# Recurrence of an RWKV-7 layer on one core: chain in two sets of eight heads, state update in two accumulating parts

## What is computed

```python
def step(S, inp):
    r_t, d_t, k_t, v_t, a_t, b_t = inp
    sa = jnp.einsum('bhij,bhj->bhi', S, a_t)
    S = (S * d_t[:, :, None, :] + sa[..., None] * b_t[:, :, None, :]
         + v_t[..., None] * k_t[:, :, None, :])
    return S, jnp.einsum('bhij,bhj->bhi', S, r_t)
```

## Time and profile before

| | us |
|---|---|
| median of 3 runs | 1520.93 (1519.63 to 1522.9) |
| profiled execution, its own time | 1519.45 |
| span of its trace | 1517.7 |
| TensorE busy | 1413.9 (93%) |
| VectorE busy | 928.3 (61%) |
| ScalarE busy | 754.1 (50%) |
| mean granted TensorE clock | 0.958 |
| recurrence, first sb to last y | 140.62 to 273.51 |

### The profile page before, as it was taken

One profiled execution on the slowest core, in us unless ns is written; L12 is line 12 of the kernel. 1 busy time (PEld: TensorE's weight loads), 2 busy tenths in 40 slices (PEclk: granted clock), 3 DMA queues, 4 the chain that ended last, 5 costly groups with the idle time before them and its releaser, 6 DMA issues.

```text
span 1517.7 us, 27277 instructions
## 1 busy us (share of the span) xinstructions
PE 1413.9 (93%) x11109; PEld 1266.0 (83%) x11109; DVE 928.3 (61%) x1355; ACT 754.1 (50%) x1166; POOL 43.9 (3%) x79
## 2 busy tenths in 40 slices
PE   5988988789999898899998999999999998899998
PEld 4867988379999787799997898799997787789997
DVE  6847332666676757666767465755557566565554
ACT  4562321165555755655557464544445464454443
POOL 5000000010000000000000000010001000000000
PEclk9998988599999999999999999999999999999999
DMA  7420001455555440555554554556654543245550
GB/s 221 135 103 1 4 3 44 166 155 193 188 172 194 142 168 25 186 203 193 167 193 147 186 185 148 164 174 191 193 187 146 178 165 102 84 159 180 190 191 29
DMA packets 135073, 222.25 MB, mean 146 GB/s; under 512 B 6137, under 2 KB 105697, under 8 KB 134720
## 3 DMA queue, kind: packets, MB, share of 16 engines
q1 hardware_dynamic: 132688, 214.19, 43.4%
q0 software_dynamic: 2144, 6.61, 1.4%
q10 hardware_dynamic: 144, 0.06, 0.0%
HBM read 219.77 MB, written 1.05 MB: 145 GB/s over the span
## 4 chain that ended last, share of the span: by engine, by line
PE 84%; DVE 9%; ACT 5%; issue 2%; DMA 1%; SPq 0%; DVEq 0%; ACTq 0%
PE ps L477 81%; DVE ulo L463 1%; ACT uhi L455 1%; DVE scratch L1799 1%; PE ps L771 1%; DVE x_sb L1773 1%; DMA raw<-in_w_rkv 1%; PE ps L1082 0%; DVE scratch L2087 0%; DVE xn_lo L1761 0%; DVE xs L1749 0%; ACT scratch L1310 0%; DVE x_sb L1779 0%; PE ps L918 0%; ACT xn_hi L1341 0%
## 5 line engine op out<-in xcount | busy, mean ns | idle before, releaser
L463 DVE TENSOR_TENSOR ulo<-raw,uhi 128x1024 fp32r<-128x1024 f32 x400 | 488.3, 1224 | 383.4 <-ACT uhi L455 383.1
L455 ACT ACTIVATE uhi<-raw 128x1024 fp32r<-128x1024 f32 x400 | 422.7, 1059 | 442.8 <-PE ps L477 437.5
L477 PE MATMUL ps<-xn_hi,uhi 128*128 128x256 f32 x1472 | 418.0, 284 | 6.7 <-DVE xn_lo L1815 2.6
L477 PE MATMUL ps<-xn_lo,uhi 128*128 128x256 f32 x1472 | 416.5, 283 | 0.0
L477 PE MATMUL ps<-xn_hi,ulo 128*128 128x256 f32 x1472 | 416.4, 283 | 0.0
L477 PEld LDWEIGHTS ps<-xn_hi,uhi 128*128 128x128 f32 x1472 | 282.3, 192 | 10.5 <-issue 4.0
L477 PEld LDWEIGHTS ps<-xn_lo,uhi 128*128 128x128 f32 x1472 | 282.4, 192 | 1.7
L477 PEld LDWEIGHTS ps<-xn_hi,ulo 128*128 128x128 f32 x1472 | 282.3, 192 | 0.0
L477 PE MATMUL ps<-uhi,xm_hi 128*128 128x512 f32 x512 | 201.3, 393 | 1.8 <-DVE xm_lo L2035 1.1
L477 PE MATMUL ps<-ulo,xm_hi 128*128 128x512 f32 x512 | 200.6, 392 | 0.0
L477 PE MATMUL ps<-uhi,xm_lo 128*128 128x512 f32 x512 | 159.9, 391 | 0.0
(11 more groups left out here) (273 smaller groups left out, 1331.2 us busy)
## 6 DMA issues: line engine op xcount, KB each, us to landing
raw<-in_mlp_w SPq DMA_DIRECT2D x64, 1024.0 KB, 5.3
raw<-in_w_up SPq DMA_DIRECT2D x44, 1024.0 KB, 5.1
raw<-in_w_down SPq DMA_DIRECT2D x22, 1024.0 KB, 4.9
raw<-in_gmlp_w_in SPq DMA_DIRECT2D x16, 1024.0 KB, 5.4
raw<-in_fox_w_in SPq DMA_DIRECT2D x16, 1024.0 KB, 5.3
raw<-in_w_rkv SPq DMA_DIRECT2D x12, 1024.0 KB, 6.2
raw<-in_gmlp_w_out SPq DMA_DIRECT2D x8, 1024.0 KB, 4.8
raw<-in_w_o_rwkv SPq DMA_DIRECT2D x4, 1024.0 KB, 5.9
```

What stands on the lines that cost most here:

```text
L455: nc.scalar.activation(ring_unit(uhi, m, n), raw_unit(n, j), ACT.Copy).then_inc(hi_done, 1)
L463: nc.vector.tensor_tensor(ring_unit(ulo, m, n), raw_unit(n, j), ring_unit(uhi, m, n).bitcast(F32), ALU.subtract).then_inc(lo_done, 1)
L477: return nc.tensor.matmul(o, l, r, start=start, stop=stop, skip_group_check=True)
```

## The change

- `rs`, `ys`, `y` and `st` are cut into two sets of eight heads (g = 0, 1) as `u` was. VectorE's part of `rs` and `st` is cut likewise (four head pairs per instruction instead of eight), so each set's chain needs only its own set's results.
- `st` becomes two stages: `sv` (keys x values, needs no solution) opens the accumulation in a ring bank, and `st` (rates x solution) closes it in the same bank; only `st` is moved out.
- The list is written anew: u0 goes in after two stages of `prepare(1)` instead of five, then a part after every five; for chunks 2 and 3 a fixed order is written out, in which `sv`, `ys` and `y` of one set stand between dependent steps of the other, and y2.1 stands after u3.

The list grows from 94 stages to 113. No arithmetic is added: the matmuls are the same in number and size.

```diff
--- before.py
+++ after.py
@@ -137,19 +137,31 @@
                 [x for g in both for x in st("l2", [g]) + st("z1", [g])] + st("z2"))
 
     def advance(c):
-        first = [("rs", c, 0), ("ys", c, 0)] if c else []
-        return [first, [("u", c, 0), ("u", c, 1)], [("y", c, 0)] + ([("st", c, 0)] if c < 3 else [])]
-
-    stages = [("kn", q, 0) for q in range(4)] + [("bonus", 0, 0)] + prepare(0)
+        def both(name):
+            return [(name, c, 0), (name, c, 1)]
+
+        state = [st for g in (0, 1) for st in (("sv", c, g), ("st", c, g))]
+        return [both("rs") + both("ys") if c else [], both("u"), state + both("y")]
+
+    first = prepare(0)
+    stages = [("kn", q, 0) for q in range(4)] + [("bonus", 0, 0)] + first
     ahead = [part for c in (0, 1) for part in advance(c) if part]
     rest = prepare(1)
+    take = 2
     while rest:
-        stages += rest[:5]
-        rest = rest[5:]
+        stages += rest[:take]
+        rest = rest[take:]
+        take = 5
         if ahead:
             stages += ahead.pop(0)
-    for part in ahead + advance(2) + advance(3):
+    for part in ahead:
         stages += part
+
+    def eight(name, c):
+        return [(name, c, 0), (name, c, 1)]
+
+    stages += eight("rs", 2) + eight("sv", 2) + eight("u", 2) + eight("ys", 2) + eight("st", 2) + [("y", 2, 0)]
+    stages += eight("rs", 3) + eight("ys", 3) + eight("u", 3) + [("y", 2, 1)] + eight("y", 3)
     return stages
 
 
@@ -279,6 +291,10 @@
         ring_bank, ring_use, ring_total = {}, {}, [0] * 4
         turn = 0
         for k, st in enumerate(stages):
+            if st[0] == "st":
+                n = stage_no[("sv", st[1], st[2])]
+                ring_bank[k], ring_use[k] = ring_bank[n], ring_use[n]
+                continue
             ring_bank[k], ring_use[k] = [], []
             for _ in range(CORE_BANKS.get(st[0], 1)):
                 b = turn % 4
@@ -920,31 +936,33 @@
                 else:
                     n, hh, c = i // 2, halves[i % 2], slice(64 * i, 64 * i + 64)
                     if name in ("rs", "ys"):
-                        wait_moved(("st", i - 1, 0))
+                        wait_moved(("st", i - 1, g))
                         if name == "rs":
-                            for q in range(2):
-                                wait_moved(("rv", n, q))
+                            wait_moved(("rv", n, g))
                         else:
                             pe.wait_ge(core_ps, stage_no[("yk", n, 1)] + 1)
-                        for j in range(8):
+                        for j in range(4 * g, 4 * g + 4):
                             for u in range(2):
                                 oo = o[u] if name == "rs" else bank(2 * n + u)
                                 last = mm(oo[hh, HD * j:HD * j + HD], (at_ if name == "rs" else rt)[halves[u], j, c],
                                           S0[halves[u], j, :], name == "rs", name == "rs")
                     elif name == "u":
                         wait_moved(("z2", n, g))
-                        wait_moved(("rs", i, 0) if i else ("rv", n, g))
+                        wait_moved(("rs", i, g) if i else ("rv", n, g))
                         for e in range(8):
                             head = 8 * g + e
                             last = mm(o[0][hh, HD * e:HD * e + HD], core_kept(n, g, "TT")[hh, e // 2, e % 2, :],
                                       by_head(core_u(n))[hh, head, :], True, True)
                     else:
-                        for q in range(2):
-                            wait_moved(("u", i, q))
-                            wait_moved(("tok" if name == "st" else "sb", n, q))
+                        if name != "sv":
+                            wait_moved(("u", i, g))
+                        else:
+                            for q in range(2):
+                                wait_moved(("tok", n, q))
                         if name == "y":
-                            pe.wait_ge(core_ps, stage_no[("ys", i, 0) if i else ("yk", n, 1)] + 1)
-                        for j in range(8):
+                            wait_moved(("sb", n, g))
+                            pe.wait_ge(core_ps, stage_no[("ys", i, 1) if i else ("yk", n, 1)] + 1)
+                        for j in range(4 * g, 4 * g + 4):
                             for u in range(2):
                                 head = 2 * j + u
                                 hc = slice(HD * head, HD * head + HD)
@@ -954,8 +972,10 @@
                                     last = mm(oo, core_kept(n, j // 4, "ArbT")[hh, j % 4, u, :], U, False, True)
                                 else:
                                     oo = o[0][halves[u], HD * j:HD * j + HD]
-                                    mm(oo, core_tok(n, 1)[hh, hc], V, True, False)
-                                    last = mm(oo, core_tok(n, 0)[hh, hc], U, False, True)
+                                    if name == "sv":
+                                        last = mm(oo, core_tok(n, 1)[hh, hc], V, j == 4 * g, False)
+                                    else:
+                                        last = mm(oo, core_tok(n, 0)[hh, hc], U, False, True)
                 last.then_inc(core_ps, 1)
 
             for st in stages[5:]:
@@ -1923,18 +1943,20 @@
                     continue
                 if name == "rs":
                     hh = slice(64 * (i % 2), 64 * (i % 2) + 64)
+                    js = slice(4 * g, 4 * g + 4)
                     for u in range(2):
-                        r = by_pair(core_u(i // 2))[hh, :, u, :]
-                        TT(r, r, by_head(o[u])[hh], ALU.add).then_inc(moved[ring_bank[k][u]], 1)
+                        r = by_pair(core_u(i // 2))[hh, js, u, :]
+                        TT(r, r, by_head(o[u])[hh, js], ALU.add).then_inc(moved[ring_bank[k][u]], 1)
                     continue
                 o8 = by_head(o[0])
                 if name == "st":
-                    scale = eS[:, :, i:i + 1].to_broadcast([P, 8, HD])
+                    js = slice(4 * g, 4 * g + 4)
+                    scale = eS[:, js, i:i + 1].to_broadcast([P, 4, HD])
                     if i == 0:
-                        ins = TT(S0, o8, scale, ALU.mult)
+                        ins = TT(S0[:, js], o8[:, js], scale, ALU.mult)
                     else:
-                        step(TT(S0, o8, S0, ALU.add))
-                        ins = TT(S0, S0, scale, ALU.mult)
+                        step(TT(S0[:, js], o8[:, js], S0[:, js], ALU.add))
+                        ins = TT(S0[:, js], S0[:, js], scale, ALU.mult)
                 else:
                     dst, a = {"x1": ("X", "X"), "x2": ("X", "X"), "x3": ("Z", "X"), "z1": ("Z1", "Z"),
                               "z2": (None, "Z1")}[name]
```

## The result

| | before | with the change |
|---|---|---|
| median of 6 runs, us | 1520.85 (1519.56 to 1523.7) | 1508.56 (1506.34 to 1511.07) |
| ratio, 95% interval | | 0.9915 (0.990 to 0.993) |
| profiled execution, own time | 1519.45 | 1509.0 |
| its span | 1517.7 | 1507.3 |
| list of stages | 94 | 113 |

By the medians the kernel is 12.3 us faster; 1508.0 was forecast. The two profiled executions differ by 10.4 us of span. All of that lies between VectorE's first piece of sb1.0 and its first of the normalisation (from here on **the stretch**): 188.78 to 273.51 before, 188.85 to 263.05 now. Behind it the same 26.4 us pass, and the rest of the program takes as long as before.

A forecast was written before the change was run, and what follows sets the result against it. It took TensorE's recurrence chain, its pauses and the half-clock stretches after them, as the bound. -5.8 + 1.1 - 9.3 = -14.0 gave 1505.4, as median 1506.9; 1.1 given back made 1508.0, range 1503.0 to 1516.0 (own case 1503.5 to 1512).

The forecast's parts named there:

- What bounds it, and how it reaches the end: Recurrence up to 273.51: TensorE's chain bounds it; time saved there passes whole through the 26.4 us behind.
- Term A: First slow stretch, after 193.54: u0 moved into earlier pauses leaves the path and TensorE's clock stays up, -5.8 us.
- Term B: Middle, st0 to y1: same work in twice the stages, one new pause ahead of rs1.1, +1.1 us, bounds 0 and 2.2.
- the instruction pause: TensorE's 1.92 us stop at 237.63 inside xn1.1, taken for late instructions: kept unchanged, bounds -1.9 and +1.9 us.
- rival 1: TensorE's clock falls as it did, so only u0's move and shorter pauses gain: -5.1 us, 1515.8, chance 0.14.
- Term C: Chunks 2 and 3: 23.8 us become 14.5 at full clock with 1.2 us of pauses left, -9.3 us.
- VectorE's half pieces: VectorE's 64 x 256 pieces of rs taken at 0.4 us each; the upper end would add 1.0 us.
- The 19 added stages at nothing: The added stage ends, each with a semaphore increment and up to four waits, cost nothing; by the skill 0.5 us.
- 2 (the halves don't overlap): Each of 19 added stages stands exposed for 0.94 us: +3.9 us, 1524.8, slower than before, chance 0.05.
- 3: u0 waits for its bank until VectorE drained sb1.1, so the first slow stretch stays: -8.2 us, 1512.7, chance 0.06.
- 4: Nothing reaches the end, because the projection behind the recurrence waits for a load instead: 1521, chance 0.03.
- The signs: Clock 1.00 from 193; chunks 2 and 3 in 14 to 16 us; L1961 near 259.5; 26.4 behind; 1.1 pause before rs1.1.

The follow-up runs named there:

- u0_early: The kernel before with only u0.0 and u0.1 moved to after two stages of the second half's preparation instead of five: median 1515.92 us, ratio 0.9987.
- rows_late: The changed kernel with POOL's three row loads into gb issued after stage u3.0 instead of yk1.1: median 1503.06 us, ratio 0.9883 to the kernel before.
- rows_late_before: The kernel before with only POOL's three row loads into gb moved from yk1.1 to after u3.0: median 1515.27 us, ratio 0.9966.
- u0_late: The changed kernel with u0.0 and u0.1 put back behind five stages of preparation: median 1508.79 us, ratio 0.9926 to the kernel before.
- plain_tail: The changed kernel with chunks 2 and 3 in the old order, still cut into sets: median 1510.36 us, ratio 0.9933 to the kernel before.
- pads: The kernel before with 104 products by a zero matrix (208 records) put in TensorE's pauses: median 1511.79 us, ratio 0.9942.

## Why the prediction was right, and where it was off

- **What bounds it, and how it reaches the end.** Right. 10.5 us went in the stretch of the profiled execution, and the 26.4 us behind it passed on all but 0.1.
- **Term A, -5.8.** By the trace right: from VectorE's drain to the end of a2, 188.78 to 206.3 before and 188.85 to 200.3 now, 6.0 us less. The assumption under it, that the clock stays up over what is left of the pauses, held in four traces with an early u0 and failed for 3.4 us in a fifth (u0_early). In the medians of runs the term is not confirmed: u0_early can't be told from no change, and u0_late isn't slower than the changed kernel.
- **Term B, +1.1.** From a2's end to rs2.0 it is 43.1 us before, 48.6 now: +5.5. Its own part was about right, though the one pause that it is added up from is 0.77 us and not 1.1: with the loads moved away in both kernels, the middle takes 42.2 us (rows_late) against 40.9 (rows_late_before), +1.3. The failing step is the one on **the instruction pause**, "I keep it": it grew by 1.3 us, and the step said nothing of the clock behind it. TensorE was busy 5.8 of 6.8 us at 0.50; at 24 ns of every 54 that is 2.6 us more, 3.9 us together. The bound (+1.9) had only the pause in it, though the first paragraph of the prediction says that a pause costs twice. The prediction's one argument on that clock (under rival 1) was that it had stayed up over the 1.92 us; it did so over 3.01 us in u0_early too, but not over 3.24 here, 3.04 in u0_late, 2.96 in plain_tail and 2.65 in pads. What decides that stays open. That the pause comes from the loads could have been read ahead: the queues' packets are in the same trace.
- **Term C, -9.3.** 24.1 us before, 14.1 now: -10.0. Two pauses of 0.40 and 0.43 remain, 0.8 us where 1.2 were taken. But the prediction gave the gain to the order of the stages as much as to the cutting; the order is worth 0.6 us by the traces.
- **VectorE's half pieces, 0.4 taken.** Right:

```profile
249.75 0.73 DVE L1949 TENSOR_TENSOR scratch<-scratch,ps 64x256 f32<-64x256 f32 x2
```

- **The 19 added stages at nothing.** Right: chunks 2 and 3 take 14.1 us less 0.8 of pauses, which is the 13.3 us of their records alone, and in rows_late TensorE is busy 64.36 of 67.84 us over all of the stages. The Trainium skill ("TensorE: Matmul & The Clock Gate", "The cost: per-tile semaphore tail") names 26.3 ns for each increment. The trace shows none of it; here each increment stands behind 16 records or more.
- **The rivals.** 1 (the clock falls as it did) is out by the trace. 2 (the halves don't overlap) is out: plain_tail has the halves back to back, with nothing open behind u2 and u3, where 0.94 stood before, and 0.40, 0.26 and 0.25 us elsewhere. 3 and 4 are out.
- **The sum.** -14.0 against -10.5 measured in the profiled pair; 3.9 us are the instruction pause and its slow stretch, 0.5 more went in the middle, and A and C gave 0.9 more. So the profiled execution took 1509.0 where the sum gave 1505.4. That the median, 1508.6, lies 0.6 us from the forecast is in part luck: the 1.1 us given back had another reason, and the executions of one kernel differ by 5 us.
- **The range.** Its upper end, 1512, isn't the sum of the terms named for it: 1508.0 + 1.0 + 1.1 + 1.9 + 2.0 is 1514.0. The result lies inside either.
- **The signs.** Three of them held: chunks 2 and 3 in 14.1 us, 26.4 us behind, and a pause ahead of rs1.1, if a shorter one. Two did not, both for the instruction pause: the clock was at 0.50 for 6.8 us, and the normalisation starts at 263.05 instead of near 259.5.

## What to carry to other kernels

Where a chain of short steps leaves TensorE in pauses, price the clock behind each pause as well as the pause, and look first for any independent work, even half of the same chain, to lay in it. Here cutting the chain into two independent sets was most of the gain in its part; the finer order added little. A pause in the middle of a stage that waits for nothing is a reason to look at the queues' packets: here a burst of loads held up the instructions, and moving three loads was worth 4 to 5.5 us, where the order's fine points gave 0.6.

## What the runs showed that I had not expected

- Instruction fetches can be held up by loads: 8.6 us between two q8 packets instead of some 3.6, while three loads of 512 KB were under way, TensorE empty for 3.24 us, gone when the loads were elsewhere or apart. The Trainium skill ("Trainium Kernel Development and Optimization", "Key Constraints") says that DMAs issued from the SP, ACT and POOL queues run on the same 16 engines and interleave; it doesn't speak of the instruction queue there. The profile here counts both kinds of packets on the same 16 engines, and the runs show that a fetch doesn't get in between such loads soon enough. In what way it is held up isn't shown.
- TensorE's clock fell after pauses of 0.48 and 0.94 us and stayed up over 0.58 and 0.67 us in the changed kernel, but also over single pauses of 1.92 us before and 3.01 us in u0_early. The length of a pause alone doesn't tell. 208 records of multiplying by zero kept it up and made the kernel 7.7 us faster.
- The same order and waits gave slow stretches of different length: 10.2 us before, 6.9 us in rows_late_before.
